# Half of the modulation blocks of an attention stage taken into the matrix inverses of an RWKV mixer, on one Trainium2 core

## The reference

```
for i in range(2):
    m_lat = split(silu(c) @ ada_w[i] + ada_b[i], 6)     # 6 x 2048 modulation values
    hn = modulate(rms_norm(h, norm1_g[i]), m_lat[0], m_lat[1])
    layer 0: p = hn @ mix_in_w                          # latent and context
             y = concat(diff_attention(p[:, :3072]), rwkv7_mixer(p[:, 3072:])) @ mix_out_w
    layer 1: y = conformer_conv(hn)
    h = h + m_lat[2] * y
    h = h + m_lat[5] * squared_relu_mlp(modulate(rms_norm(h, norm2_g[i]), m_lat[3], m_lat[4]))
```

## Time and profile before

| | us |
|---|---|
| median of 3 runs | 3133.6 (3133.14 to 3151.87) |
| the profiled execution | 3133.81 |
| its span in the profile | 3132.0 |
| attention, 606 to 742 of the span | 136 |
| mixer, 742 to about 1214 | 472 |
| one pass of the mixer (a mean of passes 3 to 6) | 57.8 |

### The profile page before, as it was taken

One profiled execution on the slowest core, in us unless ns is written; L12 is line 12 of the kernel. 1 busy time (PEld: TensorE's weight loads), 2 busy tenths in 40 slices (PEclk: granted clock), 3 DMA queues, 4 the chain that ended last, 5 costly groups with the idle time before them and its releaser, 6 DMA issues.

```text
span 3132.0 us, 52077 instructions
## 1 busy us (share of the span) xinstructions
PE 2950.7 (94%) x21870; PEld 2420.1 (77%) x21870; DVE 2135.2 (68%) x2657; ACT 1274.0 (41%) x1578; POOL 377.5 (12%) x534
## 2 busy tenths in 40 slices
PE   4899999877998998999999999999889999999999
PEld 2588987635777776888888888899757888888887
DVE  3587776567777875578878888669955655555554
ACT  2322222165555553344444444456443433434342
POOL 1000000002354341012122121000000000000000
PEclk8799999988999998999999999999989999999999
DMA  9986887793000033678888888655335555565553
GB/s 328 350 292 221 307 310 263 254 350 113 23 13 15 23 70 135 191 269 296 285 292 298 293 294 298 206 182 179 122 94 175 190 191 187 192 192 189 192 178 131
DMA packets 306023, 640.73 MB, mean 205 GB/s; under 512 B 19035, under 2 KB 23937, under 8 KB 303585
## 3 DMA queue, kind: packets, MB, share of 16 engines
q1 hardware_dynamic: 269280, 529.94, 50.2%
q0 software_dynamic: 28384, 94.76, 9.2%
q10 hardware_dynamic: 8128, 12.72, 1.1%
HBM read 623.81 MB, written 13.40 MB: 203 GB/s over the span
## 4 chain that ended last, share of the span: by engine, by line
PE 85%; DVE 7%; DMA 4%; ACT 2%; issue 2%; ACTq 0%; SPq 0%; DVEq 0%
PE ps L467 46%; PE ps L506 15%; PE ps L508 8%; DMA raw<-in_ada_w_dram 3%; PE ps L486 2%; PE ps L1807 1%; PE ps L2613 1%; PE ps L1955 1%; PE ps L404 1%; PE ps L1907 1%; DVE rw_mt L1489 1%; DVE rw_mb L1487 1%; DVE rw_scc L1470 1%; PE ps L3165 1%; PE ps L1691 1%
## 5 line engine op out<-in xcount | busy, mean ns | idle before, releaser
L444 DVE TENSOR_TENSOR split_lo<-raw,split_hi 128x2048 fp32r<-128x2048 f32 (+1 forms) x372 | 849.3, 2286 | 468.2 <-ACT split_hi L432 460.3
L432 ACT ACTIVATE split_hi<-raw 128x2048 fp32r<-128x2048 f32 x368 | 702.1, 1913 | 1082.4 <-PE ps L467 750.0
L506 PE MATMUL ps<-xa,split_hi 128*128 128x512 f32 x2048 | 721.0, 397 | 4.2 <-ACT xa L665 4.2
L508 PE MATMUL ps<-xa,split_lo 128*128 128x256 f32 x2048 | 573.0, 280 | 0.0
L506 PEld LDWEIGHTS ps<-xa,split_hi 128*128 128x128 f32 x2048 | 385.1, 188 | 98.0 <-ACT xa L665 4.5
L467 PE MATMUL ps<-split_hi,hT_hi 128*128 128x512 f32 x992 | 387.1, 390 | 0.0
L508 PEld LDWEIGHTS ps<-xa,split_lo 128*128 128x128 f32 x2048 | 386.8, 189 | 0.2
L467 PE MATMUL ps<-split_hi,hT_lo 128*128 128x512 f32 x992 | 386.0, 389 | 0.0
L467 PE MATMUL ps<-split_lo,hT_hi 128*128 128x512 f32 x992 | 386.0, 389 | 0.0
L467 PEld LDWEIGHTS ps<-split_hi,hT_hi 128*128 128x128 f32 x992 | 186.2, 188 | 40.2 <-issue 1.8
L467 PEld LDWEIGHTS ps<-split_hi,hT_lo 128*128 128x128 f32 x992 | 186.2, 188 | 39.0
(11 more groups left out here) (436 smaller groups left out, 4600.6 us busy)
## 6 DMA issues: line engine op xcount, KB each, us to landing
raw<-in_mlp_w_dram SPq DMA_DIRECT2D x256, 1024.0 KB, 5.6
raw<-in_ada_w_dram SPq DMA_DIRECT2D x64, 1024.0 KB, 9.0
raw<-in_mix_in_w_dram SPq DMA_DIRECT2D x48, 1024.0 KB, 5.9
raw<-in_conv_pw_w_dram SPq DMA_DIRECT2D x48, 1024.0 KB, 5.3
gate<-in_ada_w_dram SPq DMA_DIRECT2D x172, 256.0 KB, 4.9
line<-in_ada_w_dram POOLq DMA_DIRECT2D x171, 256.0 KB, 5.0
late<-in_ada_w_dram POOLq DMA_DIRECT2D x85, 256.0 KB, 5.0
tmpa<-in_ada_w_dram SPq DMA_DIRECT2D x84, 256.0 KB, 4.8
```

The source lines that it names most:

```text
L432: nc.scalar.activation(split_hi[:, c, :, 0:n], raw[:, c, :, 0:n], ACT.Copy).then_inc(hi_done, 1)
L444: nc.vector.tensor_tensor(split_lo[:, c, :, 0:n], raw[:, c, :, 0:n], split_hi[:, c, :, 0:n], ALU.subtract).then_inc(lo_done, 1)
L506: pe.matmul(ps[:, base + j, :], split_hi[:, c, kk, j * P:(j + 1) * P], both, start=(k == 0), stop=False, skip_group_check=True)
L508: mm = pe.matmul(ps[:, base + j, 0:SEQ], split_lo[:, c, kk, j * P:(j + 1) * P], xa_hi[:, k, :], start=False, stop=(k == KT - 1), skip_grou ...
```

## The change

The attention keeps four blocks (8 to 11), half a block a head, and its PE order is spread over all heads: chunk 2n and 2n + 1 of the row of 16 chunks go into head n, one before and one after the turned maps. ACT's `act_ada` runs in heads 1, 3, 5 and 7 only.

Blocks 12 to 15 become eight halves of 256 columns, one a pass of the mixer. A half's weights come in four chunks of 0.5 MB (`send_ada_half`). PE multiplies it in eight pieces of 128 columns (`pe_ada_piece`: four matmuls, 8 records each), piece k - 2 right after update k, for k = 2 to 9, into PSUM bank 1. ACT copies the half and sends it to memory (`act_ada_half`) between its last `level_values` and its first `own_blocks`. The scan, whose first products use bank 1, waits for that copy. `mix_out`'s first weights are now sent chunk by chunk as the last pass's half is used.

```diff
-ADA_A, ADA_T = 8, 1
+ADA_A, ADA_T, ADA_X = 8, 4, 8
...
+        def send_ada_half(sp, x):
+            src = a["ada_w"][0].rearrange("(p k) n -> p k n", k=KT)[:, :, half_col(x):half_col(x) + SEQ]
+            for c in range(NCH):
+                sp.wait_ge(pe_ada, (Q_MIX + x - 1) * 4 + (c + 1))
+                sp.dma_start(raw[:, c, :, 0:SEQ], src[:, c * CHUNK:(c + 1) * CHUNK, :]).then_inc(raw_in[c], 16)
+
+        def pe_ada_piece(pe, x, bank, i):
+            c, o = i // 2, i % 2 * P
+            if i % 2 == 0:
+                pe.wait_ge(raw_in[c], (Q_MIX + x + MIX_M) * 16 + 16)
+            for kk in range(CHUNK):
+                mm = pe.matmul(ps[32 * kk:32 * kk + 32, bank, o:o + P], s32[:, c * CHUNK + kk, :], raw[:, c, kk, o:o + P],
+                               start=(i == 0), stop=(c == NCH - 1), skip_group_check=True)
+            if i % 2:
+                mm.then_inc(pe_ada, 1)
+
+        def act_ada_half(act, x, bank):
+            q = Q_MIX + x
+            act.wait_ge(pe_ada, q * 4 + 4)
+            act.wait_ge(ada_st, 16 * (ADA_T + x))
+            nc.scalar.activation(part[:, x % 2, 0:SEQ], ps[:, bank, 0:SEQ], ACT.Copy).then_inc(ada_part, 1)
+            act.wait_ge(ada_part, q + 1)
+            act.dma_start(mod_d[0, :, half_col(x):half_col(x) + SEQ], part[0:P:32, x % 2, 0:SEQ]).then_inc(ada_st, 16)
...
                 for k in range(1, NS):
                     if k < NT_DVE:
                         update(x, k)
+                    if 2 <= k < NT_DVE:
+                        if k == 2:
+                            free_of_scores(x, ADA_BANK)
+                        pe_ada_piece(pe, x.off, ADA_BANK, k - 2)
                     if k in (2, 3):
                         opened_corner(x, k - 2)
...
+                pe.wait_ge(ada_part, Q_MIX + x.off + 1)
                 mm = inputs_of(x, 0)
...
                     if 0 < n < HEADS:
-                        weights(n, 0)
-                        weights(n, 1)
+                        weights(2 * n)
                     if n:
                         maps_turned(n - 1)
                     if n < HEADS:
-                        weights(n, 2)
+                        weights(2 * n + 1)
...
                     if n + 1 < HEADS:
                         turned(n + 1)
-                    if n < HEADS:
-                        weights(n, 3)
```

More of the change, by code:

```diff
@@ L139 @@
 Q_AT = ADA_A
-Q_ALL = Q_AT + ADA_T * HEADS
+Q_MIX = Q_AT + ADA_T
+Q_ALL = Q_MIX + ADA_X
 SCAN = [[0, 1, 2, 3], [1, 0, 3, 2]]
@@ L406, in pe_ada_chunk, with half_col @@
             mm.then_inc(pe_ada, 1)
+        def half_col(x):
+            return (Q_AT + ADA_T) * NB + x * SEQ
+        def send_ada_half(sp, x):
[19 more added lines that the diff above has]
+            act.dma_start(mod_d[0, :, half_col(x):half_col(x) + SEQ], part[0:P:32, x % 2, 0:SEQ]).then_inc(ada_st, 16)
         def pe_ada_columns(pe, q):
@@ L957, in build_trunk @@
         FIRST_PREP = [2, 7, 2, 7, 2, 7, 2, 7, 2]
+        ADA_BANK = 1
         def prep_bank(x, n):
@@ L1215, in inverse @@
                         gate_values(x.last())
+                act_ada_half(act, x.off, ADA_BANK)
                 own_blocks(x, 0)
@@ L2140, in pool_rest @@
             stage_end(pool, 3)
-            pool.wait_ge(ada_st, 16 * HEADS)
+            pool.wait_ge(ada_st, 16 * (ADA_T + ADA_X))
             pool.wait_ge(mrow_st, 16 * ADA_M)
@@ L2709, in _ @@
             sp.wait_ge(lo_done, 4 * MIX_M)
-            with sp.Fori(0, HEADS) as i:
+            with sp.Fori(0, ADA_T) as i:
                 q = i + Q_AT
                 send_ada(sp, 0, i * NB + Q_AT * NB, ("ada", q - 1))
+            for x in range(ADA_X):
+                send_ada_half(sp, x)
             sync_rest(sp)
@@ L2897, in attention @@
                         first_exponentials()
-                    if n < HEADS:
-                        act_ada(act, 0, (n + Q_AT) * NB, n + Q_AT, 0, n * 16, 0)
+                    if n < HEADS and n % 2:
+                        b = n // 2
+                        act_ada(act, 0, (b + Q_AT) * NB, b + Q_AT, 0, b * 16, 0)
                     if n == HEADS - 1:
@@ L3141, in scores, with weights @@
                               A["kT"][h * HD:(h + 1) * HD, :], start=True, stop=True).then_inc(at_sc, 1)
-            def weights(i, c):
+            def weights(n):
+                i, c = n // NCH, n % NCH
                 pe_ada_chunk(pe, i + Q_AT, i + (Q_AT + MIX_M), c, 0, i + Q_AT)
@@ L3178, in attention @@
                 pe.wait_ge(mrow_ok, ADA_M)
-                weights(0, 0)
-                weights(0, 1)
+                weights(0)
                 pe.wait_ge(mix_ev_a, evacuated(MIX_M - 1, 1))
```

## The result

The changed kernel took 3164.5 us (median of 19 runs, 3149.2 to 3181.7) beside 3142.2 us of the kernel before (19 runs, 3126.7 to 3158.2): ratio 1.0077, with a 95% interval of 1.0057 to 1.0097. I had said 3131.5 us, and a range that ends at 3147. By the bound of 1% it is still "no change", but the sign is wrong and the time lies outside the range. My base was low as well: the 3133.8 us that I started from stood for three runs, and 19 runs of the same kernel have their median at 3142.2. The profiled execution of after took 3172.5 us (span 3170.4), 38.4 us more of span than the one of before.

The account below looks back on a forecast made before the run. Bounds: in the attention, DMA for early heads, then each head's own chain; in the mixer's inverse, a relay between DVE and PE. 3133.8 - 12.3 (attention) + 10.0 (mixer) = 3131.5 us, range 3120 to 3147.

Parts of the forecast that it names:

- at the full clock: Mixer: PE busy 50 of 54 us at a granted clock of 1.00, read from the windows.
- rival A: Attention: with 16 chunks fewer PE waits longer before the values, which run at 3.34 us; saves 4.5, 3139.3 us; chance 0.18.
- to head 2's scores: Attention, head 1 to head 2: 4.3 us from the block copy going, 2.2 from quicker stores; together 6.5 us saved.
- head 2 to head 3: Attention: period falls from 17.7 to 12.9 us, the head's own chain remaining; 4.8 us saved.
- the rest: Attention, head 3 to the end of head 7, 64.0 us: PE's chunk behind the turned queries goes; about 1 us saved.
- DMA waits gone: Attention, sign in the profile after: DMA share near 0.6 and no PE idle time that ends with `raw`.
- Piece 0.35: Mixer: one piece of 8 records of 128 columns takes PE 0.35 us, bounds 0.27 and 0.59.
- With a piece 1.33, against DVE's 1.37: Mixer's inverse, from step 4: update 0.98 us, with a piece 1.33, within DVE's step of 1.37, so it just fits.
- rival B: Mixer's inverse: PE becomes the bound at updates 4 to 8; 8 x 2.8 with a 0.59 piece, 3145.5 us; chance 0.18.
- The three places on PE's path: Mixer: pieces behind updates 2 and 3 and between updates 8 and 9 each cost 0.35, 1.05 us a pass.
- the copy's 0.2: Mixer: ACT's `act_ada_half` delays its `own_blocks` and `half_product`; 0.2 us a pass, 1.1 if nothing hid it.
- Rival C: Mixer: pieces fit, 0.17 us each, 0.5 us a pass, copy nothing; 3125.5 us; chance 0.22.

Follow-up runs that it names:

- e6: Changed kernel plus full-width matmuls nobody reads in PE's gaps at the inverse's end, three after the first last update, two after the second; 3144.4 us, ratio 1.002.
- e12: Kernel before plus five full-width matmuls nobody reads, one after each of updates 3 to 7, none at the inverse's end; 3198.9 us, ratio 1.0167.
- e13: Kernel before plus full-width matmuls nobody reads after updates 3 to 7 and in the inverse's end gaps (1, 2, 2); 3145.7 us, ratio 1.0007.
- e9: Kernel before with the change's attention part alone (blocks 12 to 15 left out), plus five full-width unread matmuls in the inverse's end gaps; 3128.6 us, ratio 0.9955.
- e5: Kernel before plus five full-width matmuls nobody reads in PE's idle gaps at the inverse's end (1, 2, 2); 3132.3 us, ratio 0.997.
- e7: Changed kernel with pieces moved: after updates 4 to 7, two after update 9, two after the first last update; ACT's copy behind `own_blocks`; 3139.5 us, ratio 0.9994.
- e15: Kernel before plus five narrow unread groups (four matmuls, 32 columns of weights), one after each of updates 3 to 7, none at the end; 3164.4 us, ratio 1.0079.
- e8: As e7, with two full-width matmuls nobody reads added in the last gap before the corners; 3140.7 us, ratio 1.0004.
- e10: As e6, but each added filler is a narrow group of four matmuls with 32 columns of weights; 3155.4 us, ratio 1.004.
- e11: Changed kernel, pieces after updates 4, 5, 6 (two), 7, three after 9; copy moved; full-width unread matmuls after both last updates (1, 2); 3131.9 us, ratio 0.9966.
- e14: Kernel before plus two full-width matmuls nobody reads, only in the last gap before the corners; 3134.3 us, ratio 0.9976.
- e1: Changed kernel's attention part alone: blocks 12 to 15 left out, no pieces, copies or weight loads in the mixer; 3139.6 us, ratio 0.9985.

## Why the prediction was wrong

**The step that failed is the clock in the mixer.** I read 1.00 in one window of one pass, wrote "at the full clock", and priced the mixer at it for all eight passes. None of the rivals had the mixer's clock in it; rival A had put the danger of a colder PE into the attention alone. The inverse's last 4 us hold idle times of 0.56, 0.95 and 0.70 us around matmuls of 32x32 tiles; the rows stood in the trace, and I passed over them. More windows of before alone wouldn't have warned me: all of its passes 0 to 6 stand at 1.00, and only the last, at 0.81, shows that the mixer's clock can fall. Of after's +24.3 us in the means (3166.2 less 3141.9) the lost clock is 19.6. That filling the gaps undoes it is shown by e6 (-21 us in the means, the clean pass unchanged) and, from the other side, by e12 and e13.

**The attention.** In the two profiles I was close, step by step: to head 2's scores -6.7 (said -6.5), head 2 to head 3 -4.1 (-4.8), the rest +0.8 (-1), together -10.0 against -12.3; DMA waits gone, as said. But one profile of before is a poor base. From head 0's first turned rows (607.95 in before's trace) to the first `opened` the nine traces with the attention of before have 145.8 to 149.2 us, mean 147.3, and mine was the longest, so that the steps came out close is in part luck; the eight with the new one have 138.9 to 146.2, mean 142.0. The term is about -5; e9 against e5 says -3 to -5. That is near rival A's 4.5, but A isn't borne out by it. Its first half came: PE waits up to 3.8 us for `at_pT`. Its second didn't: the values take 3.39 us at 703.65, but before had three as slow, and the granted clock of the stage is 0.84 against 0.85.

**The pieces.** Piece 0.35: right (0.355). "With a piece 1.33, against DVE's 1.37 ... a piece fits, just": wrong by 0.1, as an update holds PE 1.08 us when what follows isn't a corner. PE needs 1.44 a step and is the bound from update 4 on, which is rival B's mechanism at less than half its price: 0.37 us from update 4 to update 8, where B had 0.2 a step. The three places on PE's path cost 0.50, 0.50 and 0.35. Together 1.70 a pass, 13.6 in all, against 10.0 with the copy; the copy's 0.2 is 0. Rival C (0.17 a piece) is out.

**Sum, redone:** from 3142 and not 3133.8, -5 + 13.6 + 15 to 20 of clock gives 3142 + 24 to 29; measured 3166.2 in the mean. Without the clock it would be +8.6, slower all the same, by this estimate: the pieces cost more in the places they were given than the attention gained. e7 shows what the places cost: 1.35 us a pass.

**The rule on idle gaps.** The section on why this matters for your kernels (the Trainium skill, TensorE: Matmul & The Clock Gate) I had cited for the attention. The same page, in the section on a second HAM failure mode, tells of another kernel, in which PE idled briefly and often between groups of matmuls and the clock swung between its two levels. The traces agree in part, for the mixer: no idle time of PE in after's passes 0 to 6 exceeds 1.23 us, and the stretches at 1.2 GHz are there. But before had idle times of up to 1.08 us in its passes 1 to 6 and no such stretch there. Had I weighed that rule it would have been a fifth case on the slower side.

**What stays open.** Why e12 and e15 fall in every pass, while before, with the same gaps, fell in none of passes 0 to 6 of its profile. The regular row of e12 (62, 62, 74) speaks for something in how the thin stretch comes round in time, which I didn't vary by itself. The halts in the last pass (e8, e10, e11) are open too, what they wait for and in how many runs they come; they are a rival for what these three lost beside e5 and e6. So is how much of the lost clock lies outside the mixer. That the fillers work through the clock is shown by clocks and times together; through what property of theirs (width, count, place) is shown only so far: two wide ones in the last gap nearly suffice (e14).

## What to carry to other kernels

Look at the granted clock over every pass and over several runs before pricing a stage "at the full clock", and list PE's idle times in the thinnest stretch: here it fell right behind that, and one fall (3 or 15 us) outweighs many careful tenths. Matmuls of full width that nobody reads, put only where PE waits anyway, can be worth more than the work one tries to hide: five of them a pass, or two, took some 8 us off this kernel. Measure them in their place, as in e12 five of them cost over 50. If real work is to be hidden, put it into PE's waits first (1.35 us a pass here), not evenly over the steps.

## What the hardware did unexpectedly

- Once low, the clock stayed low for whole scans although PE was busy for 35.3 of 36 us (after, e1, e12). Short stretches (10 us windows at 0.66) cost 3 us, long ones 15.
- Five added matmuls of 0.4 us a pass, in steps where PE waited 0.2 us, cost over 50 us (e12); five more at the end of the inverse took 53 of them away (e13).
- In the last pass PE stopped for 2.2 to 3.0 us with nothing in the profile to wait for, in three kernels with added matmuls at the end of the inverse (e8, e10, e11), and the clock was at 1.2 GHz for over 20 us after it. e13 had a halt of 2.1 us, too, earlier in its last pass, and its clock held there.
- A group of 8 records over four column groups takes 0.36 us with 128 columns and 1.07 with 512: a third of it and not a quarter.
